# Forming every third weight chunk's low part with an adding DMA instead of a VectorE subtraction

## The reference: what is computed

```
xn = rmsnorm(h) ; proj = xn @ w_in                       # 2048 x 7936
q, k, v attention (8 heads) and latent attention (8 heads, w_uq, w_ukv)
h = h + (sigmoid(g_a) * (y_a @ w_branch_a) + sigmoid(g_b) * (y_b @ w_branch_b)) @ w_out
hn = rmsnorm(h) ; h = h + (silu(hn @ w_gate) * (hn @ w_up)) @ w_down        # 5632 wide
x = rmsnorm(h)
m = sliding-window attention(rms_norm(x) @ swa_w_in) @ swa_w_out ; x = x + rms_norm(m)
x = x + rms_norm((silu(conv(h @ up_gate)) * conv(h @ up_val)) @ ffn_w_down)
```

## Time and profile before

| | |
|---|---|
| median of 2 runs | 2370.88 us |
| the profiled execution | 2369.46 us, of which span 2367.7 us |
| TensorE busy (matmul) | 2346.6 us, 99% of the span |
| VectorE busy | 1437.1 us, 61% |
| ScalarE busy | 1149.5 us, 49% |
| GpSimd busy | 23.9 us, 1% |
| DMA | 439.25 MB, queues busy 62% of 16 engines' span |
| mean granted TensorE clock | 0.998 |

### The profile page before, as it was taken

How to read it: one execution, slowest core, us unless ns; L and a number is a source line. 1 busy time by engine, 2 the same in 40 slices (tenths; PEclk the granted TensorE clock), 3 DMA queues, 4 the chain that set the end, 5 groups by cost and what they waited for, 6 DMA issues and landing times.

```text
span 2367.7 us, 28497 instructions
## 1 busy us (share of the span) xinstructions
PE 2346.6 (99%) x11298; PEld 1963.7 (83%) x11298; DVE 1437.1 (61%) x2039; ACT 1149.5 (49%) x1704; POOL 23.9 (1%) x35
## 2 busy tenths in 40 slices
PE   8999999999999999999999999999999999999998
PEld 7888888888888888888888887788888888888886
DVE  6445565665554454454444566657888888885444
ACT  6445454545444444444444566655544444444442
POOL 1000000000000000000000100000000000000000
PEclk9999999999999999999999999999999999999999
DMA  7666555655666666666666665455666666666564
GB/s 261 187 187 175 156 174 152 186 185 181 195 187 189 193 188 188 193 188 205 191 191 190 209 197 163 131 151 179 188 193 189 189 193 188 189 193 191 192 194 151
DMA packets 226420, 439.25 MB, mean 186 GB/s; under 512 B 13632, under 2 KB 17888, under 8 KB 225904
## 3 DMA queue, kind: packets, MB, share of 16 engines
q1 hardware_dynamic: 224400, 429.51, 60.5%
q0 software_dynamic: 1888, 7.93, 1.1%
HBM read 435.24 MB, written 2.15 MB: 185 GB/s over the span
## 4 chain that ended last, share of the span: by engine, by line
PE 97%; ACT 1%; DVE 1%; issue 0%; DMA 0%; POOL 0%; DVEq 0%; ACTq 0%; POOLq 0%
PE bank L1357 24%; PE bank L1359 24%; PE bank L1358 24%; PE bank L1387 14%; PE bank L1389 7%; PE bank L1399 2%; PE bank L1543 1%; PE bank L1564 1%; PE bank L1442 0%; ACT whi L605 0%; PE bank L1459 0%; PE bank L1540 0%; PE bank L1565 0%; PE bank L1444 0%; ACT JK L597 0%
## 5 line engine op out<-in xcount | busy, mean ns | idle before, releaser
L906 DVE TENSOR_TENSOR wlo<-raw,whi 128x1024 fp32r<-128x1024 f32 (+1 forms) x812 | 988.1, 1218 | 883.3 <-ACT whi L605 882.6
L605 ACT CAST whi<-raw 128x1024 fp32r<-128x1024 f32 (+1 forms) x812 | 847.4, 1044 | 1158.7 <-PE bank L1359 907.0
L1357 PE MATMUL bank<-whi,TT 128*128 128x512 f32 (+1 forms) x1488 | 591.2, 397 | 3.2 <-DVE wlo L906 3.1
L1359 PE MATMUL bank<-whi,TT 128*128 128x512 f32 (+1 forms) x1488 | 578.2, 389 | 0.0
L1358 PE MATMUL bank<-wlo,TT 128*128 128x512 f32 (+1 forms) x1488 | 577.4, 388 | 0.0
L1387 PE MATMUL bank<-TT,whi 128*128 128x512 f32 x1408 | 488.9, 394 | 0.8 <-DVE TT L1147 0.7
L1389 PE MATMUL bank<-TT,wlo 128*128 128x256 f32 x1408 | 390.1, 277 | 0.0
L1357 PEld LDWEIGHTS bank<-whi,TT 128*128 128x128 f32 x1488 | 279.9, 188 | 62.1 <-DVE wlo L906 4.0
L1358 PEld LDWEIGHTS bank<-wlo,TT 128*128 128x128 f32 x1488 | 280.1, 188 | 58.1 <-issue 2.9
L1359 PEld LDWEIGHTS bank<-whi,TT 128*128 128x128 f32 x1488 | 279.6, 188 | 58.1
L1387 PEld LDWEIGHTS bank<-TT,whi 128*128 128x128 f32 x1408 | 264.0, 188 | 62.5 <-issue 1.3
(11 more groups left out here) (211 smaller groups left out, 1586.6 us busy)
## 6 DMA issues: line engine op xcount, KB each, us to landing
raw<-in_ffn_w_up_dram SPq DMA_DIRECT2D x176, 512.0 KB, 3.6
raw<-in_w_in_dram SPq DMA_DIRECT2D x120, 512.0 KB, 3.7
raw<-in_w_gate_dram SPq DMA_DIRECT2D x88, 512.0 KB, 3.7
raw<-in_w_up_dram SPq DMA_DIRECT2D x88, 512.0 KB, 3.7
raw<-in_w_down_dram SPq DMA_DIRECT2D x88, 512.0 KB, 4.7
raw<-in_ffn_w_down_dram SPq DMA_DIRECT2D x88, 512.0 KB, 4.8
raw<-in_swa_w_in_dram SPq DMA_DIRECT2D x48, 512.0 KB, 3.6
raw<-in_w_out_dram SPq DMA_DIRECT2D x32, 512.0 KB, 4.6
```

The source lines that it names most:

```text
L605: eng.copy(whi[:, t % RING, 0:a * n], raw[:, t % RAW, 0:a * n]).then_inc(s_cast, 1)
L906: eng.tensor_tensor(wlo[:, t % RING, 0:a * n], raw[:, t % RAW, 0:a * n], whi[:, t % RING, 0:a * n].bitcast(F32), ALU.subtract).then_inc(s_ ...
L1357: eng.matmul(o, lh[:, ts], hi[:, kk, :], start=start, stop=False)
L1359: mm = eng.matmul(o, ll[:, ts], hi[:, kk, :], start=False, stop=stop)
```

## The change

For every chunk t from 12 to 799 with t divisible by 3, which are 263 of the 812, the low part is formed in another way. ScalarE, right after its cast, waits for it and writes the negated high part into `wlo` (`copy` with scale -1, L612 in the new numbering). GpSimd then issues a DMA (L564) that reads the same weights once more from DRAM and adds them onto `wlo`. Three semaphores `low0` to `low2`, taken in turn, report that the adding DMAs have landed, and TensorE waits for them before such a chunk. The other 549 chunks go as before. The loads into `raw` now wait for the cast of chunk t - 4, and for its subtraction where it has one. GpSimd's program becomes a loop over the steps, so that its other work is issued between the adding DMAs.

```diff
+def low_by_dma(t):
+
+    return 12 <= t < 800 and t % 3 == 0
...
             def fetch(t):
                 _, _, k0, a, n, name, c = chunks[t]
                 if t >= RAW:
-                    sp.wait_ge(s_lo, t - RAW + 1)
+                    sp.wait_ge(s_cast, t - RAW + 1)
+                    sp.wait_ge(s_lo, dve_low[t - RAW + 1])
...
+            def add_raw(t):
+
+                _, _, k0, a, n, name, c = chunks[t]
+                po.wait_ge(s_minus, dma_low[t] + 1)
+                out = wlo[:, t % RING, 0:a * n].rearrange("p (a n) -> p a n", a=a)
+                eng.dma_start(out, w[name][:, k0:k0 + a, c:c + n], accum_op=ALU.add).then_inc(l_low[dma_low[t] % 3], 16)
...
+            for t in range(END):
+                if t + 2 < END and low_by_dma(t + 2):
+                    add_raw(t + 2)
+                for name, i in steps[t]:
+                    side(name, i)
...
                 eng.copy(whi[:, t % RING, 0:a * n], raw[:, t % RAW, 0:a * n]).then_inc(s_cast, 1)
+                if low_by_dma(t):
+                    ac.wait_ge(s_cast, t + 1)
+                    copy(wlo[:, t % RING, 0:a * n], whi[:, t % RING, 0:a * n].bitcast(F32), -1.0).then_inc(s_minus, 1)
...
             def subtract(t):
                 _, _, _, a, n, _, _ = chunks[t]
+                if low_by_dma(t):
+                    return
                 ve.wait_ge(s_cast, t + 1)
...
+            def low_part(t):
+                pe.wait_ge(s_cast, t + 1)
+                if low_by_dma(t):
+                    pe.wait_ge(l_low[dma_low[t] % 3], 16 * (dma_low[t] // 3 + 1))
+                else:
+                    pe.wait_ge(s_lo, dve_low[t + 1])
...
             def stream(t):
...
-                pe.wait_ge(s_lo, t + 1)
+                low_part(t)
...
             def stream_t(t):
...
-                pe.wait_ge(s_lo, t + 1)
+                low_part(t)
```

More of the change, by code:

```diff
@@ L362, in build @@
         s_cast, s_lo, s_mm, s_half, s_emptyA, s_emptyV = sems("cast lo mm half emptyA emptyV")
+        s_minus = sems("minus")[0]
+        l_low = sems("low0 low1 low2")
         l_xt = sems("xt0 xt1 xt2 xt3 xt4 xt5 xt6 xt7")
@@ L395, in build @@
         steps = side_steps()
+        dve_low, dma_low = [0], [0]
+        for t in range(END):
+            dve_low.append(dve_low[-1] + (not low_by_dma(t)))
+            dma_low.append(dma_low[-1] + low_by_dma(t))
         side_bank, side_before, side_last = side_banks(steps)
@@ new lines, in side @@
+            def side(name, i):
+                if name == "rs":
+                    row_rstd(i)
+            for t in range(END):
+                if t + 2 < END and low_by_dma(t + 2):
+                    add_raw(t + 2)
+                for name, i in steps[t]:
+                    side(name, i)
+                if t == 3:
+                    po.wait_ge(s_biasln, 1)
+                    eng.dma_start(lines[:, :], oh).then_inc(l_lines, 16)
+                if t == DN:
+                    po.wait_ge(s_uqtr, 8)
+                    po.wait_ge(s_mktr, 4)
+                    po.wait_ge(s_mm, DN)
+                    eng.dma_start(GB[:, :], bass.AP(A["final_norm"].tensor, 0, [[0, P], [1, D]])).then_inc(l_gf, 16)
+                if t == IN2 + 1:
+                    po.wait_ge(s_mm, IN2)
+                    po.wait_ge(l_lines, 16)
+                    po.wait_ge(s_rs, 5)
+                    eng.memset(KK[64:128, :, 0, :], 0.0).then_inc(s_kkz, 1)
+                    po.wait_ge(s_kkz, 1)
+                    eng.memset(KK[0:64, :, 1, :], 0.0).then_inc(s_kkz, 1)
+                    po.wait_ge(s_kkz, 2)
+                    load_bias(0)
+                    load_bias(1)
+                if t in (492, 508):
+                    po.wait_ge(s_pbias, 8 if t == 492 else 16)
+                    load_bias(2 if t == 492 else 3)
+                if t == 518:
+                    po.wait_ge(s_qtr, 8)
+                    eng.dma_start(GB[:, :], bass.AP(A["norm_g_2"].tensor, D, [[0, P], [1, D]])).then_inc(l_g1, 16)
+                if t == 550:
+                    po.wait_ge(s_mg, 4)
+                    sem, value = emptied_at(("post", 1), 1)
+                    po.wait_ge(sem, value)
+                    eng.dma_start(GB[:, :], bass.AP(A["norm_g_2"].tensor, 3 * D, [[0, P], [1, D]])).then_inc(l_g3, 16)
```

## The result

| | before | changed |
|---|---|---|
| median, us | 2370.88 | 3462.58 (3453.46 to 3471.7, 2 runs) |
| ratio, 95% interval | | 1.4605 (1.4439 to 1.477) |
| profiled execution, us | 2369.46 | 3453.46 |
| span, us | 2367.7 | 3451.7 |
| TensorE busy / not busy, us | 2346.6 / 21.1 | 2698.9 / 752.8 |

The kernel is 46% slower. The table splits the 1084 us that the span gained without any model. TensorE does the same 11298 matmuls and is busy for 352 us more; the other 732 us are stops: 2.78 us for each of the 263 adding DMAs. The lower clock explains some 301 of the 352 us: over the span it took (1 - 0.910) x 3451.7 = 311 us of full speed away, and summed over TensorE's busy time alone 303 us, where the kernel before lost 2. Most of the rest is a matter of booking.

What follows compares the result with a forecast made beforehand. TensorE, busy for 2346.6 of 2367.7 us, was taken to bound the kernel. The profiled 2369.5 us plus 1037 for stops and 342 for the lower clock gave 3748, forecast as 3750 us, range 2700 to 5000.

Steps and rivals of the forecast that it cites:

- Cover and chain: Before every third chunk: a chain of 9.75 us against a two-chunk cover of 5.81, so TensorE stops 3.94 us.
- the stop does not shorten by running ahead: Chunks t + 1 and t + 2 are ready early, but the cast of t + 3 starts only at the end of t.
- The landing, 7.5 us: Issue to landing of the adding DMA, the chain's large term: 7.5 us, the middle of the 1 MB rows without the longest.
- the bytes read are those of a 1 MB load: Reason for 7.5 us: the adding DMA reads 512 KB of weights and 512 KB of wlo.
- GpSimd's start, 0.1 us, and 0.02 to the first matmul: Two small chain links: GpSimd starting the DMA, 0.1 us, and from landing to TensorE's first matmul, 0.02 us.
- +1037: Total for TensorE's stops: 263 chains of 9.75 us, 2564, less the 1527 us of the stretch they replace.
- The clock, +342 us: Most stops bring TensorE's clock down and chunk t pays 1.3 us of an estimated 1.6, 263 times.
- Loads not on the path: Loads of raw do not delay the chain: with adding DMAs the DMA engines need 8.8 us of each 14 us.
- not slower: Rival: the cover hides the whole chain if the adding DMA lands within 3.56 us; 2371 us, chance 4%.
- Cheap: Rival: second read overlaps the first, landing 3.7 to 5.2 us; 2593 us at 4.4, 2803 at 5.2, chance 14%.
- Slow work: Rival: DMA engines add slowly, landing 10 us or more; 4486 us at 10, 5144 at 12.5, chance 25%.

Runs made afterwards that it cites:

- filling the stops: Changed kernel, with 12 zero-weight matmuls on TensorE before it waits for an adding DMA (not in a group's first chunk): 3315.65 us.
- the adding DMAs alone: Changed kernel without negation, VectorE forming every low part; adding DMAs go to a buffer nobody reads, only GpSimd waits for them: 2414.07 us.
- four buffers and the late wait: Changed kernel with 4 buffers for whi and wlo, 3 for raw, and the DMA wait behind the eight high-part matmuls: 2494.7 us.
- late wait: Changed kernel, but in the 263 chunks TensorE does the eight high-part matmuls before waiting for the adding DMA: 2946.93 us.

## Why the prediction was right, and where its terms were off

The time, 3463 us for a forecast of 3750 and a range of 2700 to 5000, came by the mechanism that was forecast.

- **Cover and chain**: right. The negation took 1.06 us as taken from the activation of the same shape, and the chain of waits shows the links in the order given. That the stop does not shorten by running ahead is seen in the period above, and the cover of two chunks is shown by moving it: a chunk more, or eight matmuls more, takes the stops down.
- **The landing, 7.5 us**: the term that was mis-sized; it measured 5.9, and the difference is 421 us of the sum. The step that failed is "the bytes read are those of a 1 MB load". The engines do spend 2.0 times as long on an adding DMA as on a load, as was argued, but the landing does not go with the bytes: half of them is 0.6 us, the whole second read and addition 0.9. The middle of the 1 MB rows was the wrong neighbour: 5.9 us lies between the quickest of them, 5.2, and that middle, and a plain DMA of the same size and queue, which no row had, took 5.0.
- **GpSimd's start, 0.1 us, and 0.02 to the first matmul**: 0.29 and 0.14, which is 82 us more. With the landing that corrects +1037 to +698, and the 0.08 us from release to cast make it +719; measured were 732, or 774 with the 0.16 us of each stop that is booked as busy. What is left goes with the use of medians: the mean landing was 6.0 us.
- **The clock, +342 us**: 301, or 1.15 us per stop and not 1.3. That it is on the path is shown by filling the stops. That most stops bring it down by the same 1.6 us is not how it came about: some chunks ran wholly at 0.50 and others not at all, so that the sum came out near is in part luck. That TensorE was busy for 352 us more looks like a closer hit than it is.
- **Loads not on the path**: right for the changed kernel (they waited in one place, 0.9 us), and at full pace the adding DMAs alone cost at most 11 us outside the norms. But the loads share in the landing, and with four buffers and the late wait casts wait 115 us for them.
- **The rivals**: "not slower" would need a landing of 3.56 us, and the shortest of 263 was 4.9. "Cheap" needed 5.2 or less in the median. "Slow work" needed 10. The formula of the Trainium skill, "DMA: Bandwidth & Descriptors", section Anatomy of one DMA, gives 3.2 us for 512 KB, an estimate, against 5.9 here and 5.0 without addition; its slope gives 0.6 us for 256 KB, also an estimate, the same number as halving showed, though beside other loads, and its fixed part is not what was measured. The Trainium skill, "Collectives: The Full Stack", section on why ReduceScatter is half of AllGather, has two source reads for a reduction and so half the rate. The engines' time bears this out in part: 2.0 times a load of SyncE's queue, but 3.26 us against 2.01, 1.6 times, where only the addition differs.

## What to carry to other kernels

Taking work off an engine that nobody waits for gains nothing, and what is put in its place must fit under the same cover: count the buffers, multiply by the time of a chunk, and lay the whole new chain beside it, the landing above all. Where it doesn't fit, one more buffer gave the most here, 769 us of the 1092. A later wait gave 516 and halving the transfer 528: the one moves the cover by 1.8 us but let the landing grow by 0.6, the other moves the landing by only 0.6 but also halves the negation ahead of it. And when a stop is periodic, add the clock: stops of 2.8 us in the mean cost 0.4 of their length again here in slower matmuls.

## What the runs showed of the hardware

- An adding DMA of 512 KB onto SBUF landed in 5.9 us, a plain one from the same queue in 5.0, an adding one of 256 KB in 5.3. GpSimd's own part was 1.19, 0.72 and 0.86 us, and the 16 DMA engines were held for 3.26, 2.01 and 1.46 us.
- The landing varied more with what ran beside it than with its own size: the same DMA took 5.9, 6.5, 7.2, 7.4 and 7.6 us in five kernels, in which the loads of `raw` moved at 131, 133, 151, 149 and 167 GB/s between its issue and its landing (medians). Letting TensorE get on sooner (the later wait, the fourth buffer) made it longer each time, which gave back part of the gain.
- Fewer adding DMAs had longer ones: 5.9 us with every third chunk, 7.2 with every sixth.
- Stops of 2.78 us in the mean cost 1.15 us each in lower clock (changed kernel), stops of 4.0 us 2.1 (every sixth chunk), stops of 1.5 us 0.5 (late wait). A stop also adds 0.16 us to TensorE's busy time at full clock.
